# Closing a layer with the last four value tiles multiplied by token half, and the casts of the next weights moved behind squares, a copy and the roots

## The reference

```python
out = einsum('chk,chkd->cd', gelu(act) * gate, v_tab[idx])   # expert values
x_lat = x_lat + mod_lat[5] * out                             # residual
# then: the next layer's norm and input product, or the final norm
```

## Time and profile before

| | |
|---|---|
| median of 3 runs | 1839.9 us |
| the profiled execution | 1837.93 us |
| its span in the trace | 1836.1 us |
| TensorE busy | 1822.6 us, 99% of the span |
| TensorE weight loads busy | 1584.0 us, 86% |
| DVE busy | 1520.1 us, 83% |
| ACT busy | 966.7 us, 53% |
| POOL busy | 454.0 us, 25% |
| mean DMA rate | 205 GB/s |

### The profile page before, as it was taken

How to read it: one execution, slowest core, us unless ns; L and a number is a source line. 1 busy time by engine, 2 the same in 40 slices (tenths; PEclk the granted TensorE clock), 3 DMA queues, 4 the chain that set the end, 5 groups by cost and what they waited for, 6 DMA issues and landing times.

```text
span 1836.1 us, 35178 instructions
## 1 busy us (share of the span) xinstructions
PE 1822.6 (99%) x11716; PEld 1584.0 (86%) x11716; DVE 1520.1 (83%) x2819; ACT 966.7 (53%) x1631; POOL 454.0 (25%) x229
## 2 busy tenths in 40 slices
PE   8999999999999999999999999999999999999998
PEld 7999988888888888888889998888888888888887
DVE  6775889989998888888888589998999888885555
ACT  6754455665555444445555545565555544445554
POOL 6046588950000000000000368893000000000000
PEclk9999999999999999999999999999999999999999
DMA  9866455556554555588874455556655555555553
GB/s 383 330 237 220 161 187 191 184 199 218 203 179 163 182 172 176 186 308 320 323 254 161 161 170 184 191 185 207 218 194 171 171 173 174 180 172 194 193 190 132
DMA packets 104327, 376.40 MB, mean 205 GB/s; under 512 B 12481, under 2 KB 12737, under 8 KB 104001
## 3 DMA queue, kind: packets, MB, share of 16 engines
q1 hardware_dynamic: 103248, 373.11, 59.1%
q0 software_dynamic: 432, 2.10, 0.3%
q10 hardware_dynamic: 576, 0.32, 0.1%
HBM read 374.43 MB, written 1.05 MB: 204 GB/s over the span
## 4 chain that ended last, share of the span: by engine, by line
PE 91%; DVE 4%; DMA 2%; ACT 1%; POOL 1%; issue 0%; SPq 0%; ACTq 0%; DVEq 0%; POOLq 0%
PE ring L1882 22%; PE O L1935 13%; PE O L1937 13%; PE O L1936 13%; PE ring L1880 6%; PE ring L1887 6%; PE ring L1844 3%; PE ring L1587 2%; PE ring L1588 2%; PE ring L1589 2%; DMA raw<-in_u 2%; PE ring L1870 2%; PE ring L1849 1%; PE O L1870 1%; DVE wL L959 1%; ACT wH L574 1%
## 5 line engine op out<-in xcount | busy, mean ns | idle before, releaser
L574 ACT ACTIVATE wH<-raw 128x1024 fp32r<-128x1024 f32 x597 | 633.3, 1061 | 789.6 <-DMA raw<-in_v 361.6
L959 DVE TENSOR_TENSOR wL<-raw,wH 128x1024 fp32r<-128x1024 f32 x384 | 470.1, 1224 | 171.0 <-ACT wH L574 166.2
L1882 PE MATMUL ring<-hX,wH 128*128 128x512 f32 x1984 | 482.6, 393 | 0.0
L1882 PEld LDWEIGHTS ring<-hX,wH 128*128 128x128 f32 x1984 | 362.0, 188 | 69.5 <-issue 0.7
L1935 PE MATMUL O<-wH,gateH 128*128 128x512 f32 x1024 | 402.3, 393 | 0.2
L1937 PE MATMUL O<-wH,gateL 128*128 128x512 f32 x1024 | 398.9, 390 | 0.0
L1936 PE MATMUL O<-wL,gateH 128*128 128x512 f32 x1024 | 398.5, 389 | 0.0
L526 POOL TENSOR_TENSOR wL<-raw,wH 128x1024 fp32r<-128x1024 f32 x128 | 321.3, 2519 | 46.7 <-ACT wH L574 45.7
L1937 PEld LDWEIGHTS O<-wH,gateL 128*128 128x128 f32 x1024 | 192.2, 188 | 40.7
L1936 PEld LDWEIGHTS O<-wL,gateH 128*128 128x128 f32 x1024 | 192.4, 188 | 39.2
L1935 PEld LDWEIGHTS O<-wH,gateH 128*128 128x128 f32 x1024 | 192.3, 188 | 39.2 <-DVE gateL L1459 0.6
(11 more groups left out here) (227 smaller groups left out, 2469.4 us busy)
## 6 DMA issues: line engine op xcount, KB each, us to landing
raw<-in_u SPq DMA_DIRECT2D x256, 512.0 KB, 3.2
raw<-in_v SPq DMA_DIRECT2D x256, 512.0 KB, 3.3
ada_v<-in_ada SPq DMA_DIRECT2D x40, 512.0 KB, 4.4
raw<-in_w_q SPq DMA_DIRECT2D x30, 512.0 KB, 3.2
ada_m<-in_ada SPq DMA_DIRECT2D x24, 512.0 KB, 5.2
raw<-in_w_in SPq DMA_DIRECT2D x23, 512.0 KB, 4.3
ada_f<-in_ada SPq DMA_DIRECT2D x16, 512.0 KB, 15.1
raw<-in_w_out SPq DMA_DIRECT2D x16, 512.0 KB, 3.6
```

The lines of the kernel that those rows point to most:

```text
L574: nc.scalar.activation(wH[s % RAW][:, :], (place or raw[s % RAW])[:, :], ACT.Copy).then_inc(s_h, 1)
L959: nc.vector.tensor_tensor(wL[s % RAW][:, :], raw[s % RAW][:, :], wH[s % RAW][:, :].bitcast(fp32), ALU.subtract).then_inc(s_low, 1)
L1882: ins = mm(bank[:, :], wH[s][:, k * P:k * P + P], hX[:, k, :, :].rearrange("p two t -> p (two t)"), start=(not low_weights_first and k == ...
```

## The change

On TensorE the last four value tiles are now multiplied by token half: token half 0 of all four tiles first, then token half 1 of tile 124, the eight transposes of token half 0 in one piece, token half 1 of tiles 125 and 126, four means, and token half 1 of tile 127. On ACT, in layer 0, the cast of `p_in` tile 0 moves behind the eight squares of token half 0, the cast of tile 1 behind the copy of token half 1, and the cast of tile 2 behind the two roots. On DVE the two subtractions that belong to tiles 0 and 1 move behind the residuals of token half 0 and of token half 1.

```diff
@@ act: norm(n) @@
                 if n % 2:
                     split_high(BASE["w_q", n // 2], 0, 2)
+                elif n < NORMS - 1:
+                    split_high(BASE["p_in", 1], 0, 2)
@@ act: the close @@
                 ahead_gated(31, 0)
-                if layer < LAYERS - 1:
-                    ahead(base, 31, 1)
...
                 nc.scalar.activation(otok[:, 0, 0:512], O[0][:, :], ACT.Copy).then_inc(s_oc_a, 1)
+                for j in range(KT):
+                    square_half(0, j)
+                if layer < LAYERS - 1:
+                    ahead(base, 31, 1)
+                act.wait_ge(s_pe, base + EXP_TILES)
+                nc.scalar.activation(otok[:, 1, 0:512], O[2][:, :], ACT.Copy).then_inc(s_oc_a, 1)
                 if layer < LAYERS - 1:
                     ahead(base, 31, 2)
-                for j in range(5):
-                    square_half(0, j)
-                act.wait_ge(s_pe, base + EXP_TILES)
-                nc.scalar.activation(otok[:, 1, 0:512], O[2][:, :], ACT.Copy).then_inc(s_oc_a, 1)
-                for j in range(5, KT):
-                    square_half(0, j)
                 for j in range(KT):
                     square_half(1, j)
-                if layer < LAYERS - 1:
-                    ahead(base, 31, 3)
                 norm(2 * layer + 2)
@@ dve: the close @@
                     if s < 2:
                         ahead_gated(31, s)
-                    elif layer == 0 and s == 2:
-                        ahead(base, 31, s)
...
                     if tt == 1:
+                        if layer == 0:
+                            ahead(base, 31, 2)
                         dve.wait_ge(s_pe, base + EXP_TILES)
                         nc.vector.tensor_copy(otok[:, 1, 512:1024], O[3][:, :]).then_inc(s_oc_v, 1)
-                        if layer == 0:
-                            ahead(base, 31, 3)
...
+                if layer == 0:
+                    ahead(base, 31, 3)
                 norm(2 * layer + 2)
@@ tensor: the close @@
-                for s in range(2):
-                    values(31, s)
-                pe.wait_ge(s_gated, 2 * NGRP * (layer + 1))
-                for s in (2, 3):
+                for s in range(4):
                     values_ready(31, s)
                     token_values(s, 0, 0, last=(s == 3))
                     ins = token_values(s, 0, 1, last=(s == 3))
                 ins.then_inc(s_half, 1)
-                token_values(2, 1, 0)
-                turned(0, 0)
-                token_values(2, 1, 1).then_inc(s_pe, 1)
-                turned(0, 1)
+                pe.wait_ge(s_gated, 2 * NGRP * (layer + 1))
+                token_values(0, 1, 0)
+                token_values(0, 1, 1).then_inc(s_pe, 1)
+                for quarter in range(2):
+                    turned(0, quarter)
+                for s in (1, 2):
+                    token_values(s, 1, 0)
+                    token_values(s, 1, 1).then_inc(s_pe, 1)
+                for j in range(4):
+                    token_mean(0, j)
                 token_values(3, 1, 0, last=True)
                 token_values(3, 1, 1, last=True).then_inc(s_pe, 1)
-                for j in range(5):
-                    token_mean(0, j)
                 turned(1, 0)
                 turned(1, 1)
-                for j in range(5, KT):
+                for j in range(4, KT):
                     token_mean(0, j)
```

## The result

The changed kernel takes **1846.5 us** (median of 8 runs, 1844.7 to 1847.9); the kernel before, over the same sessions, 1841.1 us (8 runs, 1839.9 to 1842.6). The ratio is 1.0028, with a 95% interval of 1.0018 to 1.0037: slower by 5.2 us by the ratio, between 3.3 and 6.8 (the medians differ by 5.4). The forecast was +5.4 us on the kernel before. It was put on top of 1839.9 us, which gave 1845.3; the kernel before stands 1.2 us higher over all its runs.

What follows compares the result with a forecast made beforehand. TensorE's stream of work was taken to bound the kernel; +2.55 us in layer 0 and +2.89 in layer 1 gave +5.4 on 1837.93, 1843.4, and with 2.0 for the runs' median 1845.3 us; range 1842.8 to 1848.0.

Steps and rivals of the forecast that it cites:

- The waits: Both closes: TensorE waits for tiles 126 and 127, costing with restarts 2.01 us in layer 0, 2.18 in layer 1.
- Four means ahead of tile 127: Both closes: eight pieces of means stand before tile 127's token half 1, delaying the last value matmul by 0.89 us.
- the first transposes: Both closes: six matmuls now cover the copy TensorE waited for ahead of the transposes of token half 0, -0.18 us.
- The tail: Behind the last value matmul: transposes 0.26 us sooner, 24 pieces of means instead of 22 take 0.26 more; comes out even.
- The roots of layer 0: Layer 0: roots no longer held by tile 2's cast, -0.17 us, between 0 and -0.3.
- so nothing: Layer 0: POOL's loads of group weights and keys move later with tile 2's cast, needed only behind four p_in tiles; no cost.
- No wait for the tiles: Rival: tile 127 ready within 4.1 us of tile 123's end, waits vanish, change costs 1.2 us, 1841.1; chance 0.12.
- The casts collide: Rival, layer 0: p_in tile 1 or 0 lands late, ACT's cast delays squares and roots, +1 to +2.5 us; chance 0.09.
- The clock falls: Rival: TensorE's clock falls after new idle stretches of 0.66 and 1.41 us standing close together; chance 0.04.

Runs made afterwards that it cites:

- E2: The changed kernel, but tile 124 multiplied whole first and only tiles 125 to 127 by token half; 1844.2 us, ratio to before 1.0019.
- E8: E1 with the root's table loaded ahead of tile 123's cast, DVE's windows and modulations behind tile 127's subtraction, four means behind tile 127; 1840.3 us, ratio 1.0000.
- E3: The changed kernel, with the four means behind the last value matmul instead of ahead of tile 127's token half 1; 1844.8 us, ratio to before 1.0025.
- E6: The changed kernel, with the cast of p_in tile 2 back between the last square and the roots; 1846.7 us, one run.
- E1: The changed kernel, with tiles 126 and 127 loaded into two spare buffers halfway through the value product; 1843.8 us, ratio to before 1.0016.
- E4: The kernel before with only TensorE's new order, casts and subtractions left in their old places; 1858.7 us, one run.

## Why the prediction was right

**The waits** (forecast 1.90 and 2.07 us, with 0.11 for restarts each). The change asks for tile 127 eighteen matmuls behind tile 124, at 950.68 + 18 x 0.2266 = 954.76; it got it at 956.72: 1.96. Layer 1: 1820.71 and 1822.84: 2.13. The tile's subtraction ends as far behind tile 124's first matmul as it did before (5.90 us against 5.93 in layer 0), as argued. Two small terms were off, one each way: from the subtraction's end to TensorE's start it is 0.14 us, not 0.05, and the matmul behind it starts 0.31 later, 0.08 lost and not 0.11. TensorE kept to its order in these waits: tile 124's token half 1, whose parts it had been reading since 950.68, started only at 958.19, behind the six matmuls of tile 127. E2 takes 2.8 of the 5.4 us away with six matmuls more of lead, and E8 against E3 prices the waits at 4.1 us: they are the larger part of the cost.

The forecast took the end of that subtraction from the trace, so it did not matter for the number what the end hangs on; the text had that in part wrong. It reads the 3.44 us from the issue of tile 127's load to its cast as the load's time. The load landed 3.06 us behind its issue (1815.72), and in the rest ACT was finishing the root's table load and the gates. By these rows a faster load of tile 127 alone would have gained nothing there, and the table load moved away alone 0.25 us (an estimate).

**Four means ahead of tile 127, and the first transposes** (+0.89 and -0.18). Together with the waits the last value matmul was to come 2.72 and 2.89 us later against tile 124; it came 965.24 - 950.68 = 14.56 against 11.80, +2.76, and 14.73 against 11.80, +2.93.

**The tail.** Transposes were to start 1.08 us behind the last value matmul: they start 1.09 behind. The 24 pieces of means were to take 0.26 more than 22; they take 2.84 against 2.81. Here the choice failed. The 24 pieces start 0.111 us apart, the pace of the ten pieces in the earlier trace rows; the 22 stood 0.12 apart on average, and up to 0.147 near their end: it was before that the squares held them, and "busy without a gap" hid it. The transposes take 0.06 more to the first mean than they did. Together 0.17 us comes back in each close.

**The roots of layer 0** (-0.17, between 0 and -0.3): from the means' end to the spread it is 0.73 against 0.96, -0.23; E6 isolates 0.20.

**What the prediction missed.** It said that tile 2's cast and POOL's work behind it move later "so nothing". Beside POOL's subtraction a DVE instruction on the path to the first product of layer 1 is longer (1.73 us instead of 0.48 in the change, 1.34 in E6), and moving the work changes which one: +0.3 us (E6). Layer 0, where the tail's 0.17 and the roots' 0.06 more stand against it, came out 0.12 above its forecast, and layer 1, with the tail's 0.17 alone, 0.13 below. So the sum of 5.44 against 5.43 measured in the closes is partly luck, and more so as a trace with the longer loads would have shown up to 0.9 us more. Term by term the forecast was good to about 0.3 us.

**The rivals.** *No wait for the tiles* is out: four waits. What that case would have cost was put at 1.2 us. E8 is it with the means behind tile 127, 0.56 us shorter than before; by E3 the means ahead of it are worth 1.9, which puts the case at 1.3 (an estimate from the two, not run). Sooner loads alone don't bring it about: E1 has them and keeps two waits. *The casts collide*: they didn't. ACT in layer 0 of the change:

```profile
966.17 1.05 ACT L574 ACTIVATE wH<-raw 128x1024 fp32r<-128x1024 f32 x1
967.41 2.12 ACT L904 ACTIVATE sq<-XT 128x128 f32<-128x128 f32 x8 [0.19 <-DVE XT L1556]
```

Tile 1's cast ends at 967.22 and ACT is idle for 0.19 us before it can square: a cover of 0.2 us where 0.1 was forecast. E4 shows what late casts on this path cost. *The clock falls*: it didn't in the change; its chance of 0.04 was the author's estimate. Windows over the waits of both closes (us, PE busy, PEld, DVE, ACT, POOL, PEclk, DMA share, GB/s):

```profile
949.00:958.00 9.00, 7.47 (x33) 5.57 (x32) 6.47 (x16) 4.74 (x7) 0.00 (x0) 1.00 0.37 118
1820.00:1830.00 10.00, 8.79 (x45) 7.17 (x46) 4.50 (x11) 4.16 (x12) 0.00 (x0) 1.00 0.01 2
```

## What to carry to other kernels

Before reordering a stream of matmuls, count for each operand how many matmuls stand between the release of its buffer and its first use; an order that reaches forward over the ring pays every microsecond by which that falls short of load, cast and subtraction, and of whatever else the casting and subtracting engines do between them (in E2 a lead of 1.36 us more took 1.42 and 1.38 us off the closes). Work that fills a wait for something else is free there and costs its full length ahead of it: the eight pieces of means cost 0.04 us during the copy (E3), and 0.91 and 1.00 us ahead of tile 127. When one wait is removed, look for what had been hiding in its slack: here the loads hid a table load of 1.28 us on ACT and 1.2 us of DVE's preparation.

## What was not expected of the hardware

Behind E4's long wait TensorE's granted clock was halved, from 1.00 to 0.50. Windows of E4's layer 0, columns as above:

```profile
960.00:965.00 5.00, 0.07 (x1) 0.00 (x0) 0.29 (x1) 1.38 (x2) 0.25 (x1) 0.92 0.29 105
965.00:970.00 5.00, 4.79 (x16) 3.98 (x17) 3.16 (x10) 0.16 (x1) 1.52 (x1) 0.50 0.00 0
...
972.00:973.00 1.00, 0.00 (x0) 0.00 (x0) 0.00 (x0) 0.00 (x0) 0.00 (x0) 1.00 0.69 229
...
975.00:976.00 1.00, 1.00 (x6) 1.00 (x6) 0.00 (x0) 0.14 (x1) 0.49 (x1) 0.50 0.00 0
```

Behind 5.14 us of idling the granted clock is 0.50 from 965 to 970. From 967.40 on, matmuls of 128x512 start 0.43 us apart instead of 0.227 and are recorded at 0.63 us instead of 0.39; at 971.15 they are back at 0.39. The second wait, of 2.63 us, is followed by the same: the clock is back at 1.00 during it (972 to 973) and at 0.50 behind it (975 to 976). By the starts, these two stretches cost some 4.5 us that no wait shows (an estimate against the same matmuls in the change): 0.8 in the eight transposes and 2.0 in the value matmuls behind the first wait, 0.9 in the eight means and 0.8 in the value matmuls behind the second. In the change, with waits of 0.55 to 1.15 us by the brackets, the clock stayed at 1.00. Waits of 1.43 us and, in E1, of 1.69 us (26.07 to 27.76; the clock is 1.00 in the windows 26 to 28 and 28 to 30) went by without a fall, and waits of 5.14 and 2.63 us were followed by one. The one of 2.63 came only 3 us behind a stretch at the lower level, so it may not stand for a wait of that length by itself; waits between 1.69 and 2.63 us no run showed. The first 3.32 us of the span, ahead of TensorE's first instruction, show 1.00 in every trace, and so does what follows them; what TensorE did ahead of the span they don't show.
